# A two-block transformer in fp32 on one NeuronCore: the norms of the first block, their residuals and next inputs in PSUM banks

## The reference

```python
def rmsnorm(x, g):
    xf = x.astype(jnp.float32)
    y = xf * lax.rsqrt(jnp.mean(xf * xf, axis=-1, keepdims=True) + EPS) * g.astype(jnp.float32)
...
        h = h + rmsnorm(m @ w_out[l], norm_mix_post[l])
        u2 = rmsnorm(h, norm_mlp_pre[l])
        a = jnp.square(jax.nn.relu(u2 @ w_up[l]))
        h = h + rmsnorm(a @ w_down[l], norm_mlp_post[l])
```

## Time and profile before

| what | us |
|---|---|
| median of three runs (lowest, highest) | 2057.47 (2057.06, 2059.71) |
| the profiled execution | 2060.59 |
| its span, first to last instruction | 2058.8 |
| TensorE busy | 1983.8 (96%) |
| VectorE busy | 1216.3 (59%) |
| ScalarE busy | 889.7 (43%) |
| GpSimd busy | 1134.4 (55%) |

### The profile page before, as it was taken

The page is one execution under the profiler, slowest core; times in us unless marked ns, Lnnn a source line. Parts: engine busy times, 40 slices in busy tenths (PEclk is TensorE's granted clock), DMA queues, the critical chain, the costliest instruction groups (busy, mean ns, idle before and its releaser), DMA issues.

```text
span 2058.8 us, 25509 instructions
## 1 busy us (share of the span) xinstructions
PE 1983.8 (96%) x9428; PEld 1621.6 (79%) x9428; DVE 1216.3 (59%) x1990; ACT 889.7 (43%) x1674; POOL 1134.4 (55%) x856
## 2 busy tenths in 40 slices
PE   7999997999999899999999999999999999999997
PEld 5887886778888667777788888887787888888885
DVE  6663326333423488878675744847577675744845
ACT  4544334433333335554453443444466453443442
POOL 5345544444444376454576666555864576666553
PEclk9999998999999999999999999999999999999998
DMA  4122221223222211111223222322210223222321
GB/s 154 52 67 102 93 92 61 82 98 107 93 102 95 73 64 60 42 62 53 81 103 103 92 94 96 108 92 97 75 42 32 72 103 103 93 95 95 107 93 61
DMA packets 48653, 174.37 MB, mean 85 GB/s; under 512 B 5392, under 2 KB 5776, under 8 KB 48528
## 3 DMA queue, kind: packets, MB, share of 16 engines
q1 hardware_dynamic: 48528, 172.73, 24.5%
HBM read 170.61 MB, written 2.10 MB: 84 GB/s over the span
## 4 chain that ended last, share of the span: by engine, by line
PE 87%; DVE 10%; issue 2%; ACT 1%; DMA 0%; POOL 0%; SPq 0%; DVEq 0%; ACTq 0%; POOLq 0%
PE b L380 26%; PE b L382 25%; PE b L381 25%; PE b L402 2%; DVE ra L464 2%; PE b L394 1%; PE b L414 1%; PE b L415 1%; PE b L413 1%; PE b L432 1%; DVE h L700 1%; DVE fa L554 1%; PE b L423 1%; DVE h L656 1%; PE b L395 1%
## 5 line engine op out<-in xcount | busy, mean ns | idle before, releaser
L235 POOL TENSOR_TENSOR ra<-raw,ra 128x512 fp32r<-128x512 f32 x632 | 884.4, 1407 | 780.9 <-ACT ra L276 779.2
L380 PE MATMUL b<-ra 128*128 128x512 f32 x2528 | 1006.0, 398 | 36.8 <-DVE ra L464 23.3
L382 PE MATMUL b<-ra 128*128 128x512 f32 x2528 | 988.5, 391 | 0.0
L381 PE MATMUL b<-ra 128*128 128x512 f32 x2528 | 988.2, 391 | 0.0
L276 ACT ACTIVATE ra<-raw 128x512 fp32r<-128x512 f32 x632 | 390.4, 626 | 527.4 <-PE b L382 514.9
L380 PEld LDWEIGHTS b<-ra 128*128 128x128 f32 x2528 | 477.4, 189 | 150.2 <-issue 35.2
L382 PEld LDWEIGHTS b<-ra 128*128 128x128 f32 x2528 | 476.9, 189 | 101.7
L381 PEld LDWEIGHTS b<-ra 128*128 128x128 f32 x2528 | 478.0, 189 | 93.5
L700 DVE TENSOR_TENSOR h<-b,h 128x512 f32<-128x512 f32 x144 | 97.1, 682 | 49.7 <-PE b L382 49.1
L585 DVE TENSOR_TENSOR ra<-b,ra 128x512 fp32r<-128x512 f32 (+4 forms) x166 | 92.2, 568 | 56.8 <-ACT ra L321 37.1
L592 DVE TENSOR_TENSOR tmp<-b,rb 128x512 f32<-128x512 f32 x69 | 47.3, 690 | 127.6 <-PE b L382 127.4
(11 more groups left out here) (259 smaller groups left out, 1983.3 us busy)
## 6 DMA issues: line engine op xcount, KB each, us to landing
raw<-in_f_g SPq DMA_DIRECT2D x40, 512.0 KB, 3.5
raw<-in_f_v SPq DMA_DIRECT2D x40, 512.0 KB, 3.4
raw<-in_f_d SPq DMA_DIRECT2D x40, 512.0 KB, 3.5
raw<-in_w_up SPq DMA_DIRECT2D x32, 512.0 KB, 3.4
raw<-in_w_down SPq DMA_DIRECT2D x32, 512.0 KB, 3.5
raw<-in_p_g SPq DMA_DIRECT2D x16, 512.0 KB, 3.5
raw<-in_w_gp SPq DMA_DIRECT2D x8, 512.0 KB, 3.4
raw<-in_w_ga SPq DMA_DIRECT2D x8, 512.0 KB, 3.4
```

The lines of the kernel that those rows point to most:

```text
L235: e.tensor_tensor(wl, src, wh.bitcast(F), ALU.subtract).then_inc(*w_low.mark(n))
L380: e.matmul(ps, wh[:, c:c + 128], xh, start=start, stop=False)
L381: e.matmul(ps, wh[:, c:c + 128], xl, start=False, stop=False)
L382: last = e.matmul(ps, wl[:, c:c + 128], xh, start=False, stop=stop)
```

## The change

Five things are edited.

1. In `post_norm` the root isn't copied to `rb`: `residual_norm` multiplies y by bank 7 itself, and writes both of its results to a spare bank instead of a buffer and `h`. From that bank ScalarE makes the high part of the next input and then copies the new `h` to SBUF; VectorE makes the low part from the same bank, behind that copy. The spare banks are three that no product uses then.
2. Ahead of the first norm the square reads the bank directly and comes ahead of the copy of y.
3. For the norms with `two=True` (the two of `post_norm` that scale y, and the last of the kernel) the eighth square is not added to `ssq`: the row `columns` has eight matmuls instead of four, the second four over that square, summed in the same four columns.
4. The four tiles of block 0 of the up-projection are copied out of their banks by ScalarE without the root; `relu` then works in place in SBUF when the root is there. Blocks 1 to 7 are as before.
5. In `outputs` of the differential attention stages a and b become one stage of four heads and eight tiles of 12 matmuls; its weights are laid out accordingly. `outputs` of the last layer stays as it was.

The rank of the norm of y goes from -3 to -2.

```diff
         elif kind == "columns":
-            src, made, free = a[0], a[1], a[2]
-            for t in free + made:
-                w.wait_ge(*t)
-            for i in range(4):
-                x = e.matmul(m.banks[STB][:, i:i + 1], src[:, 128 * i:128 * i + 128], m.ones[:, 0:1],
-                             start=True, stop=True)
+            parts, free = a[0], a[1]
+            for t in free:
+                w.wait_ge(*t)
+            for k, (src, made) in enumerate(parts):
+                w.wait_ge(*made)
+                for i in range(4):
+                    x = e.matmul(m.banks[STB][:, i:i + 1], src[:, 128 * i:128 * i + 128], m.ones[:, 0:1],
+                                 start=k == 0 and i == 0, stop=k == len(parts) - 1 and i == 3,
+                                 skip_group_check=True)
             x.then_inc(*stat.mark(n))
...
         elif kind == "residual_norm":
-            z, y, hk, gain, rb, y_done, free = a
+            b, y, hk, gain, rb, y_done, free = a
+            ps = banks[b][:, :]
             w.wait_ge(*rb)
             w.wait_ge(*y_done)
             for t in free:
                 w.wait_ge(*t)
-            e.tensor_tensor(z, y, m.rb[:, :], ALU.mult).then_inc(*els.mark((n, 0)))
+            e.tensor_tensor(ps, y, banks[STB][:, :], ALU.mult).then_inc(*els.mark((n, 0)))
             w.wait_ge(els, (n, 0))
-            e.scalar_tensor_tensor(out=hk, in0=z, scalar=gain, in1=hk, op0=ALU.mult,
+            e.scalar_tensor_tensor(out=ps, in0=ps, scalar=gain, in1=hk, op0=ALU.mult,
                                    op1=ALU.add).then_inc(*els.mark(n))
         elif kind == "relu":
-            z, b, rb, free, mm_done = a
-            w.wait_ge(*mm_done)
+            z, src, rb, free, made = a
+            w.wait_ge(*made)
             w.wait_ge(*rb)
             for t in free:
                 w.wait_ge(*t)
-            e.scalar_tensor_tensor(out=z, in0=banks[b][:, :], scalar=0.0, in1=m.rb[:, :], op0=ALU.max,
+            e.scalar_tensor_tensor(out=z, in0=src, scalar=0.0, in1=m.rb[:, :], op0=ALU.max,
...
-    def square(x, src, made):
+    def square(x, src, made, then=None):
         yield 0, "ac", lambda: (made,) if x["n"] == 0 or (x["sum"] and T.free) else None
         x["n"] += 1
         if x["n"] == 1:
             x["sum"] = done("ac", "square", row("square_first", src, (made,), stat["sum_free"]))
             x["left"] = NC - 1
+            if then:
+                then(x["sum"])
             return
         i, q, free = T.get()
         s = done("ac", "square", row("square_of", q, src, made, free))
+        if then:
+            then(s)
+        if x["left"] == 1 and x["two"]:
+            launch(root(x, (i, q, s)))
+            return
...
-    def root(x):
-        yield x["rank"], "pe", lambda: None if bank_free[STB] is None else (x["sum"], *bank_free[STB])
-        v = rstd_cols(m.ssq, (x["sum"],), 1024.0, 0)
+    def root(x, more=None):
+        made = (x["sum"], more[2]) if more else (x["sum"],)
+        yield x["rank"], "pe", lambda: None if bank_free[STB] is None else (*made, *bank_free[STB])
+        v = rstd_cols(((m.ssq, x["sum"]), *([more[1:]] if more else [])), 1024.0, 0)
         stat["sum_free"] = now("pe")
+        if more:
+            T.release(more[0], *now("pe"))
         yield x["rank"], "pe", lambda: None if bank_free[STB] is None else (v, *bank_free[STB])
...
+        if x["keep"]:
+            x["rb"] = t
             return
         yield 0, "ac", lambda: (t, *stat["rb_use"])
         x["rb"] = done("ac", "act", row("copy_rb", t, stat["rb_use"]))
...
-        for z, stage in enumerate("ab"):
-            while not ready(2 * z + 1):
+        if early:
+            for z, stage in enumerate("ab"):
+                while not ready(2 * z + 1):
+                    yield "idle"
+                yield from linear_pairs(name + stage, lambda k: part(2 * z + k), 8, add, LB2)
+        else:
+            while not ready(3):
                 yield "idle"
-            yield from linear_pairs(name + stage, lambda k: part(2 * z + k), 8, add, LB2)
+            yield from linear(name + "a", 1, 4, part, 8, add, LB2)
...
-        def post_norm(gain, nxt, u_free):
-
-            yn = norm(None)
+        def post_norm(gain, nxt, u_free, spare):
+
+            yn = norm(None, rank=-2, keep=True, two=True)
             u = norm(U_A, rank=-2 if nxt[0] == "attn" else -3)
 
+            def parts(k, b, made):
+                uh, ul = u["slots"][k]
+                ps, g = banks[b][:, :], vc(nxt[0], nxt[1] + k)
+                yield 0, "ac", lambda: (made,)
+                done("ac", "high", row("input_high", uh, ps, g, (made,), u_free))
+                h_tok[k] = (done("ac", "act", row("copy_out", h[:, k, :], b, made, ())),)
+                launch(square(u, h[:, k, :], h_tok[k][0]))
+                yield 0, "v", lambda: h_tok[k]
+                n = row("input_low", (uh, ul), ps, g, h_tok[k][0], (made,), u_free)
+                u["tok"][k] = (done("ve", "low_v", n),)
+                bank_free[b] = (u["tok"][k][0], h_tok[k][0])
+
             def residual(k):
-                yield 0, "v", lambda: (yn["rb"], y_tok[k]) if yn["rb"] and len(T.free) > 2 and (
-                    k < 2 or u["tok"][k - 2]) else None
-                i, z, free = T.get()
-                v = done("ve", "elem_v", row("residual_norm", z, y_chunk(k), h[:, k, :], vc(gain, k), yn["rb"], y_tok[k],
-                                             free))
-                T.release(i, v)
-                h_tok[k] = stat["rb_use"] = (v,)
-                input_of(u, k, nxt, u_free)
+                yield 0, "v", lambda: (yn["rb"], y_tok[k], *bank_free[spare[0]]) if yn["rb"] and (
+                    bank_free[spare[0]] is not None) and (k < 2 or u["tok"][k - 2]) else None
+                b = rot(spare)
+                v = done("ve", "elem_v", row("residual_norm", b, y_chunk(k), h[:, k, :], vc(gain, k), yn["rb"],
+                                             y_tok[k], bank_free[b]))
+                bank_free[b] = None
+                launch(parts(k, b, v))
                 if k + 1 < NC:
                     launch(residual(k + 1))
+                else:
+                    bank_free[STB] = (v,)
             launch(residual(0))
             return yn, u
 
         def evac_y(yn):
             def f(j, b, tok):
-                y_tok[j] = done("ac", "act", row("copy_out", y_chunk(j), b, tok, t_heads))
-                bank_free[b] = (y_tok[j],)
-                launch(square(yn, y_chunk(j), y_tok[j]))
+                def copied(s):
+                    y_tok[j] = done("ac", "act", row("copy_out", y_chunk(j), b, tok, t_heads))
+                    bank_free[b] = (y_tok[j],)
+                launch(square(yn, banks[b][:, :], tok, copied))
...
-        yn, u2 = post_norm("mix_post", ("mlp_pre", 0), t_u_free)
+        spare = []
+        yn, u2 = post_norm("mix_post", ("mlp_pre", 0), t_u_free, spare)
...
+        spare += LB7[4:]
...
-                    yield 0, "v", lambda: (tok, u2["rb"]) if u2["rb"] and len(T.free) > 1 else None
-                    i, z, free = T.get()
-                    v = done("ve", "evac", row("relu", z, b, u2["rb"], free, tok))
-                    bank_free[b] = stat["rb_use"] = (v,)
+                    if blk == 0:
+                        yield 0, "ac", lambda: (tok,) if len(T.free) > 1 else None
+                        i, z, free = T.get()
+                        c = done("ac", "act", row("copy_out", z, b, tok, free))
+                        bank_free[b] = (c,)
+                        yield 0, "v", lambda: (c, u2["rb"]) if u2["rb"] else None
+                        v = done("ve", "evac", row("relu", z, z, u2["rb"], (), c))
+                        stat["rb_use"] = (v,)
+                    else:
+                        yield 0, "v", lambda: (tok, u2["rb"]) if u2["rb"] and len(T.free) > 1 else None
+                        i, z, free = T.get()
+                        v = done("ve", "evac", row("relu", z, banks[b][:, :], u2["rb"], free, tok))
+                        bank_free[b] = stat["rb_use"] = (v,)
...
-                yn3, u3 = post_norm("mlp_post", ("attn", 0), now("pe"))
+                yn3, u3 = post_norm("mlp_post", ("attn", 0), now("pe"), [4, 5, 6])
...
-        nx["last"] = nxt_gain is None
+        nx["last"] = nx["two"] = nxt_gain is None
```

32 lines of the change are left out of this document (18 added, 14 removed).

## The result

| | median, us | range | runs |
|---|---|---|---|
| before | 2057.66 | 2057.06 to 2059.71 | 4 |
| changed | 2039.52 | 2038.58 to 2039.75 | 4 |

The ratio is 0.9909, 95% interval 0.9892 to 0.9926: faster by 18 us. The profiled execution took 2039.75 us, 2.05 above its span. One execution of a later experiment (a_two) took 2364.5 us at a granted clock of 0.787, and no time or stage is read from it.

A forecast was written before the change was run, and what follows sets the result against it. TensorE was taken to bound the kernel, busy for 96% of the span, its idle time in four small groups of waits. Terms A to G summed to 18.9 us, giving a median of 2038.6 us, with 8 in 10 for 2034 to 2047.

The forecast's parts named there:

- A: First gap of `post_norm`, last matmul to first residual: 6.3 us instead of 10.2, gain 3.9 us.
- F: Attention's output product, 945 to 980 us: fewer waits for residual adds with merged stages; bounds 0 and 2.8, taken 2.0 us.
- E: Product behind the second gap: of 3.7 us left as waits on VectorE, 2.7 us gone.
- B: Block 0, fed by VectorE instructions that read a bank: of 2.0 us of waits, 1.5 us gone.
- C: Between blocks 0 and 1: banks freed by copies, so block 1 follows at once; gain 6.7 us.
- D: Second gap: second four columns start 0.73 us earlier and the root's copy of 0.60 goes; gain 1.3 us.
- G: Last norm: the add between square and columns goes; gain 0.8 us.
- the feeders stay the bound: Rival: low parts or bank copies still late; B, E, F give nothing, C 2 us less; 2046.8 us; 14%.
- a bank is an expensive place to write: Rival: residual instructions writing a bank take 1.7 us each, ten us lost per stage; 2062.8 us, slower; 4%.
- all given back: Rival: C's wait reappears at `w_down` or the weights; 12 us or less remain, 2057 if everything reappears; 3%.
- the clock doesn't fall: Rival: TensorE stays at 2.4 GHz through both gaps; 6.5 us more gained, 2032.1 us; 6%.

The follow-up runs named there:

- a_two: Changed kernel with the eighth square of both post norms added by VectorE again, one set of columns each; 2037.52 and 2035.99 us, no profile comparable with the others.
- b_relu: Kernel before with only block 0's outputs copied out of their banks by ScalarE; 2051.42 us, ratio 0.9959.
- a_two_b: The kernel of a_two once more (changed kernel, eighth square of both post norms added by VectorE), run for a readable profile; 2037.93 us.
- a_order: Changed kernel with each tile of the mixer's output copied out of its bank first and squared from the copy, as before; 2037.81 us.
- a_sbuf: Changed kernel with residual and next input of both post norms made in SBUF, root still read from its bank; 2037.31 us.
- a_keep: Changed kernel with ScalarE's copy of the root to `rb` back for both post norms, residuals reading that buffer; 2037.85 us.
- a_do_old: Changed kernel with the differential attention's output product in two first stages of two slices each, as before; 2041.67 us.

## Why the prediction was right

The time came out 0.9 us above the forecast, with the range 2034 to 2047. That closeness is partly luck. The terms of the first pair of profiles add up to 19.9 us (3.0 + 1.8 + 6.7 + 1.6 + 2.9 + 3.9 + 0.0) where 18.9 were forecast, 4.3 more came from three stages for which I had no term, and the start gave 3.1 back. The later set of runs has 22.0 between the medians instead of 18.1. And two terms were off in opposite directions: A was too high and F too low.

A was 0.9 too high. The step that failed is "chain 2.4": it was read from a trace in which GpSimd's split fell on the add instead, and I didn't ask where the split would fall once the add was gone. The chain took 3.3 us; square, columns and spread came out as reckoned. The trace of before had the same stretch elsewhere, ahead of the spread of E: L484 took 1.00 us at 743.39. L487 starts second and is over 0.03 us behind GpSimd's instruction. The Trainium skill, SBUF — State Buffer, "Who interferes with whom", says that a tensor_scalar can enter a two-port mode, when its operands meet the conditions of that mode, that this mode contends with GpSimd, and that whichever of the two issues first has the shared pair of ports while the other is blocked. These rows agree with it. The 3.67 us from residual to matmul stayed, as said.

Of the 3.0 us that A did bring, the rows give 1.0 to the order of copy, split and square, 1.4 to the add, 0.8 to columns at the upper level of the clock, 0.6 to the copied root, and take 0.9 away in the chain. The 0.8 of the clock belong to the profile of before and not to the edit, as b_relu shows with its 13.90 us, and I had counted them as gain. a_two_b and a_order show that the add and the order, undone one at a time, cost 0.0 and 0.1 us, because the chain then meets GpSimd's split less: the edits overlap.

B and E had the right size (1.5 for 1.8 to 2.6, 2.7 for 2.6 to 2.9), VectorE's lines came at 0.69, 0.76 and 0.74, close to the 0.69 assumed, and the last low part came 19.5 us behind the first residual where 21.0 were reckoned. The reason was too strong: a_sbuf keeps nearly all of both without the banks. The banks take 4.5 us out of the feeding, of which the stage needed about 1.4, and a_sbuf's 2.1 are enough. By a_keep and the rows of a_sbuf about half of these come from the root that is read from its bank; no run takes both away together.

C is shown from both sides (6.9 taken away, 6.7 added alone, 6.7 forecast). Of the four `relu` from SBUF to SBUF one was stretched, one of these three (min/median/max in ns; the fourth took 691), which hid under the cover, as assumed:

```profile
L668 DVE SCALAR_TENSOR_TENSOR tmp<-tmp,rb x3: 678/680/1789, 376.4 to 378.7; 128x512 f32<-128x512 f32 x3
```

L467 shows the same in one kernel: 743 ns mean reading a bank, 1171 reading `h`. This is what the Trainium skill, SBUF — State Buffer, "Who interferes with whom", says of two SBUF inputs. The higher access overhead on PSUM of the Trainium skill, Perfetto Trace Analysis, "Optimizing Scalar/DVE Operations", isn't visible in these rows: L658 averages 686 ns with a bank on both sides, and its counterpart in a_sbuf, which writes to SBUF, has medians of 674 and 678.

D was right (1.3 for 1.4 to 1.6), with the copy at 0.62 and the add at 0.7; a_two_b has 0.8 more from the clock. G was right at equal clock (0.8), and 0.0 in the first pair of profiles. F is the term that was mis-sized, 3.9 for 2.0, and its upper bound of 2.8 fell too: I took the idle share of the window for all that its waits could cost. a_do_old shows by the starts of the matmuls that four waits cost 3.84 us, of which the view shows 2.8.

Of the rivals, "the feeders stay the bound" and "a bank is an expensive place to write" are refuted by block 0 without a wait and L660 at 0.76, "all given back" by TensorE's waits from 375 to 690 us, which are the tables' 2.3 us alone, and "the clock doesn't fall" by 0.50 behind both gaps. The price of 1.15 us from which the slow bank was to decide doesn't follow from its own sum, which leaves out the slack: 21.0 + 2.7 + 16 times the extra cost reaches 30.1 + 7.35 at 0.86 more for each instruction, not at 0.46. Nothing else rests on it.

## What to carry to other kernels

Count slack before pricing a faster feeder: a cheaper instruction is worth only what the consumer was waiting, and the rest is cover. When a link of a serial chain goes, see which instruction of a neighbouring engine the next links will now meet. Price a wait by the starts of the instructions around it, since the idle time in a view can be more than a quarter too small. Cut both traces into stages by the count of matmuls: half a microsecond shows there, where launch times differ by three.

## What the runs showed of the hardware

- A VectorE instruction of four columns in SBUF that starts while GpSimd runs a 128x512 TENSOR_TENSOR ended 0.03 us behind it in both gaps shown (332.44 against 332.41, and 328.11 against 328.08), whether it had started 1.09 or 0.37 us before. In the 13 profiles of the stage table L487 (L484 before) starts at least 0.25 us ahead of the end of such an instruction 116 times, and ends 0.02 to 0.03 us behind it every time; L481, which reads a bank, does so 82 times and always takes 0.16.
- VectorE with a bank as output and one input: 0.69 us for the product of two, 0.76 for the scaled sum, never stretched in 32 instances. It isn't the output that matters: with both inputs in SBUF the product that writes to a bank takes up to 1.60 (a_keep), and with one input in a bank the one that writes to SBUF is never stretched (16 instances, 0.67 to 0.69, a_sbuf).
- Stages that were alike instruction for instruction came out at levels about 1.5 us apart, with the clock. Behind the norm near 1440 the same stretch of the program has 24 matmuls at 1.00 in the changed kernel, and in the kernel before 17 at 0.67:

```profile
1420.08:1425.08 5.00, 5.00 (x24) 4.04 (x23) 4.31 (x11) 0.00 (x0) 3.06 (x3) 1.00 0.49 147
```

```profile
1438.28:1443.28 5.00, 5.00 (x17) 4.00 (x16) 4.21 (x11) 0.00 (x0) 2.96 (x3) 0.67 0.53 156
```

What decides between the levels is open. The tables' stall shows both levels with the edits and without them. The norm near 1440 and the sliding attention show both with the edits, but the two profiles without them or with the copies alone (before, b_relu) have the slower level in both stages, so it isn't shown that their 1.5 and 1.4 us have nothing to do with the change.
